# Where the bias row of the feed-forward residual is added: VectorE behind its multiplication, or GpSimd

## The chip, the cores and the metric

The kernel runs on one NeuronCore of a Trainium2 chip. The metric is the device time of one execution in microseconds. The engines are named as the profile names them: PE is TensorE (matmul), PEld its weight loads, DVE is VectorE, ACT is ScalarE, POOL is GpSimd, SP is SyncE, which issues most DMAs.

## What is computed

Two decoder layers on 1024 tokens of 1024 features, float32. The change touches the residual that goes into the second half of each layer, the feed-forward block (FFN). The reference, cut to it:

```python
for i in range(DEPTH):                                   # DEPTH = 2
    ...                                                  # mix: pooling + gating, or short convolution
    x = layer_norm(DEEPNORM_ALPHA * x + mix, ln1_g[i], ln1_b[i])
    hid = jnp.square(jax.nn.relu(jnp.einsum('bsd,df->bsf', x, ffn_w1[i])))   # 1024 -> 4096
    x = layer_norm(DEEPNORM_ALPHA * x + jnp.einsum('bsf,fd->bsd', hid, ffn_w2[i]), ln2_g[i], ln2_b[i])
    gate = jax.nn.sigmoid(jnp.einsum('bsd,de->bse', x, ple_gate_w[i]))
    x = x + gate * jnp.einsum('bsk,kd->bsd', p[i], ple_w[i])
```

`DEEPNORM_ALPHA * x` with `x = norm * ln1_g + ln1_b` is what the tile `resid` must hold before the products with `ffn_w2` are added to it: first `resid * (alpha * gain)`, then `+ (alpha * bias)`.

## The kernel before

**Precision.** Every float32 operand of a product is split into a high part, rounded by ScalarE, and a low part, the difference, made by GpSimd (for weights) or VectorE (for activations). A product is then three matmuls: high by high, high by low, low by high (lines 1597 to 1599).

**The FFN's first product in trips.** The hidden width is worked off in 16 blocks of 256 features. Blocks 0 and 1 are computed plainly. For the blocks 2 to 15 there is one trip each, in which a block of 2 by 2 products is got from seven products instead of eight: A11, S1, A22, S2, A12, S4, S3 (the tuple `PER_TRIP`), where A22 in a trip belongs to the block before. A's take a quarter of `ffn_w1` as it is loaded (`w_raw`), S's take sums and differences of quarters (`op_sum`). Each product is 12 matmuls of 512 columns on PE.

The weight operand of each product passes these hands, four products ahead of PE (`OP_LEAD`), in five slots (`OPERANDS`):

- DVE makes the sums for S1 (line 1260) and S3 (line 1263); POOL makes those for S2 (line 942) and S4 (line 949)
- ACT rounds each operand to its high part `op_hi` (line 1087)
- POOL subtracts to get the low part `op_lo` (line 876, in `operand_low`)
- PE waits for the semaphore `op_low`, then multiplies

Behind PE, ACT copies some results out of PSUM (lines 1097, 1103, 1109), and DVE adds the rest, squares (line 1273) and forms the sums of the hidden tiles that are spilled to DRAM for the second product (lines 1288, 1312, 1314, 1316, 1278).

**What sets the order.** Each engine walks the same list of stages, made by `make_plan`, in program order, and waits on counting semaphores. Nothing is reordered at run time: what stands behind a waiting instruction on its engine waits too. POOL's order in one trip, by operands, with b the block of the products on PE: low A12(b); sum S4(b), low S2(b), low S4(b); low S3(b); low A11(b+1); low A22(b); sum S2(b+1), low S1(b+1).

**The stage "affine".** In the first eight trips of a layer, behind the product A22, one stage "affine" works on one of the eight tiles of 128 tokens of `resid` (128 partitions by 1024 columns). DVE multiplies it with the gain row (`gb_rows[:, 0, :]`, line 1461) and raises the semaphore `gained`; POOL waits for `gained`, adds the bias row (`gb_rows[:, 1, :]`, line 922) and raises `acc_ready`. On POOL this stands between low S3(b) and low A11(b+1). On DVE it stands between the fourth hidden sum (line 1288) and the addition of S2's product from PSUM (line 1292), behind which comes the sum for the next S1 (line 1260). `acc_ready` is waited for much later: by SP before it loads operands of the second product, and by DVE before the first flush into `resid`.

There are 16 such pairs, eight in each layer. The other trips, six in each layer, have none.

Of the kernel before, what the change touches and what calls it, by code (L numbers as in the profile page):

```python
# [26 lines left out]
ALU = mybir.AluOpType  # L27
# [5 lines left out]
TT = SEQ // P  # L33
# [422 lines left out]
def trunk(nc, x, p, ev_w_in, ev_pool_w, ev_pool_scale, ev_sgu_ln_g, ev_sgu_ln_b, ev_sgu_w, ev_sgu_b, ev_w_out,  # L456
# [8 lines left out]
    with ExitStack() as ctx:  # L465
# [19 lines left out]
        resid = at("resid", [P, TT, D], 0)  # L485
# [9 lines left out]
        gb_rows = at("gb_rows", [P, 2, D], 192 * K1)  # L495
# [92 lines left out]
        gained = sem("gained")  # L588
        gb_scaled = sem("gb_scaled")
        acc_ready = sem("acc_ready")  # L590
# [258 lines left out]
        @block.gpsimd  # L849
        def _(pool):  # L850
            pool.memset(ident[:, :], 0.0).then_inc(ident_step, 1)
            pool.wait_ge(ident_step, 1)
            pool.affine_select(out=ident[:, :], in_=ident[:, :], compare_op=ALU.not_equal, fill=1.0, base=0,
                               pattern=[[-1, P]], channel_multiplier=1).then_inc(ident_step, 1)
            def split_low(slab, piece, count):
                for q in range(count):
                    n = piece + q

                    pool.wait_ge(hi_split, n + 1)
                    s = slice(q * PIECE, (q + 1) * PIECE)  # L860
                    pool.tensor_tensor(w_lo[slab % 2][:, s], raw[:, n % NRAW, :], w_hi[slab % 2][:, s].bitcast(F32),  # L861
                                       ALU.subtract).then_inc(lo_split, 1)

            def operand_free(tr, j):

                if j >= OPERANDS:
                    pool.wait_ge(trip_done, tr.slot_before(j))
                else:
                    name, value = ends[trips.index(tr)]["blk0" if j < 4 else "blk1"]
                    pool.wait_ge(sem_of[name], value)  # L870

            def operand_low(tr, b, op):
                s = tr.index[b, op] % OPERANDS
                src = op_sum[s] if op[0] == "S" else None
                pool.wait_ge(op_high, tr.hi[b, op])
                pool.tensor_tensor(by_four(op_lo[s]), by_four(src) if src is not None else w1_quarter(b, op),  # L876
                                   by_four(op_hi[s]).bitcast(F32), ALU.subtract).then_inc(op_low, 1)

            def t_lows(layer, k):
                for m in range(2):  # L880
                    pool.wait_ge(t_high, 8 * layer + 2 * {0: 0, 2: 1, 1: 2, 3: 3}[k] + m + 1)
                    pool.tensor_tensor(pair_of(t_lo[k], m), pair_of(t_raw[k], m), pair_of(t_hi[k], m).bitcast(F32),
                                       ALU.subtract).then_inc(t_low, 1)

            split_low(0, 0, 4)
            pool.wait_ge(param_in, 16 * 7)

            pool.affine_select(out=ws_n, in_=ws_n, compare_op=ALU.is_ge, fill=0.0, base=0,
                               pattern=[[0, 4], [-1, P]], channel_multiplier=1).then_inc(ident_step, 1)

            def stage(st):
                if st.split_next and st.cur + 1 < n_slabs:
                    nxt = slabs[st.cur + 1]
                    split_low(st.cur + 1, st.piece, 5 if nxt[0][0] == "gate" else 4)
                if st.kind == "prep":
                    a, i = ahead[st.layer], st.item
                    k = a.slot(i)
                    pool.wait_ge(ahead_hi, a.act[i] - 1)
                    pool.tensor_tensor(hop_lo[k][:, :, :], h_raw[a.load(i)[0]][:, :, :],  # L899
                                       hop_hi[k][:, :, :].bitcast(F32), ALU.subtract).then_inc(ahead_pool, 1)  # L900
                    o = i % len(ORDER)
                    if i < len(ORDER) * PAIRS and o in SUM_OF:
                        pool.wait_ge(ahead_hi, a.act[i])
                        pool.tensor_tensor(wop_lo[k][:, :, :], w_sum[SUM_OF[o]][:, :, :],  # L904
                                           wop_hi[k][:, :, :].bitcast(F32), ALU.subtract).then_inc(ahead_pool, 1)
                if st.kind == "alpha":

                    pool.wait_ge(sem_of[st.turned[st.half][0]], st.turned[st.half][1])
                    for k in range(HT):
                        t = st.half * HT + k  # L910
                        pool.tensor_scalar(resid[:, t, :], resid[:, t, :], ALPHA, 1.0, ALU.mult, ALU.mult)\
                            .then_inc(acc_ready, 1)
                if st.kind == "stats" and st.half == 0 and st.ln % 2 == 0:

                    pool.wait_ge(gb_in, 32 * (st.ln + 2))
                    pool.tensor_scalar(gb_rows[:, :, :], gb_rows[:, :, :], ALPHA, 1.0, ALU.mult, ALU.mult)\
                        .then_inc(gb_scaled, 1)
                if st.kind == "affine":
                    for t in st.tiles:

                        pool.wait_ge(gained, st.ln // 2 * TT + t + 1)
                        pool.tensor_tensor(resid[:, t, :], resid[:, t, :], gb_rows[:, 1, :], ALU.add)\
                            .then_inc(acc_ready, 1)
                if st.kind == "thi":
                    pool.wait_ge(t_summed, 8 * st.layer + 4)
                    for k in (0, 2):
                        t_lows(st.layer, k)
                if st.kind == "t4":
                    pool.wait_ge(t_summed, 8 * st.layer + 8)
                    for k in (1, 3):  # L930
                        t_lows(st.layer, k)
                if st.kind == "step":
                    tr, j = trips[st.layer], st.item + OP_LEAD
                    if j < len(tr.seq):
                        b, op = tr.seq[j]
                        s = j % OPERANDS
                        if op == "S2":
                            operand_free(tr, j)
                            pool.wait_ge(w1_in[b % 2], w1_landed(st.layer, b))
                            pool.wait_ge(sum_by_dve, tr.sum_dve[b, "S1"])  # L940
                            s1 = op_sum[tr.index[b, "S1"] % OPERANDS]
                            pool.tensor_tensor(by_four(op_sum[s]), by_four(s1), w1_quarter(b, "A11"), ALU.subtract)\
                                .then_inc(sum_by_pool, 1)
                            pool.wait_ge(sum_by_pool, tr.sum_pool[b, "S2"])
                            operand_low(tr, b, "S1")
                        elif op == "S4":
                            operand_free(tr, j)
                            s2 = op_sum[tr.index[b, "S2"] % OPERANDS]
                            pool.tensor_tensor(by_four(op_sum[s]), w1_quarter(b, "A12"), by_four(s2), ALU.subtract)\
                                .then_inc(sum_by_pool, 1)  # L950
                            pool.wait_ge(sum_by_pool, tr.sum_pool[b, "S4"])
                            operand_low(tr, b, "S2")
                            operand_low(tr, b, "S4")
                        elif op != "S1":
                            operand_low(tr, b, op)

            for st in plan:
                stage(st)
# [207 lines left out]
        def _(dve):  # L1166
# [38 lines left out]
            def stage(st):  # L1205
# [9 lines left out]
                if st.kind == "ffn":  # L1215
                    for k in range(2):

                        dve.wait_ge(act_value, st.aval_at + k + 1)
                        t = h_tile[2 * st.half + k][:, :]
# [150 lines left out]
                if st.kind == "fold":  # L1370
                    dve.wait_ge(flushed, st.flu)
                    for k in range(HT):
                        r = resid[:, k, HALF:D]
                        dve.tensor_tensor(r, r, common[:, k, :], ALU.add).then_inc(flushed, 1)

                if st.kind in ("out", "wide"):
                    if st.kind == "wide":
                        dve.wait_ge(flushed, st.flu)
                    for k in range(2 * len(st.tiles)):
                        t, n = st.tiles[k // 2], k % 2  # L1380
                        r = resid[:, t, n * HALF:(n + 1) * HALF]
# [54 lines left out]
                if st.kind == "stats":  # L1436
# [11 lines left out]
                    for k in range(2, HT):  # L1448
                        r = resid[:, h * HT + k, :]
# [3 lines left out]
                if st.kind == "affine":  # L1453
                    for t in st.tiles:
                        if t == 0:
                            dve.wait_ge(gb_in, 32 * (st.ln + 2))
                            dve.wait_ge(gb_scaled, st.ln // 2 + 1)

                        dve.wait_ge(sem_of[st.turned[t // HT][0]], st.turned[t // HT][1])
                        r = resid[:, t, :]  # L1460
                        dve.tensor_tensor(r, r, gb_rows[:, 0, :], ALU.mult).then_inc(gained, 1)  # L1461

                if st.kind == "mix":
                    if st.half == 0 and st.blk == 0:
                        dve.wait_ge(late_in, 32)
                    for k in range(2):
                        t = tmp[:, (st.unit + k) % NTMP, :]
# [79 lines left out]
                if st.kind == "bgate":  # L1547
                    for k in range(2):
                        t = tmp[:, (st.unit + k) % NTMP, :]
# [296 lines left out]
```

## Time and profile before

| what | value |
|---|---|
| time, median of 3 runs | 2288.95 us (2286.92 to 2289.67) |
| time of the profiled execution | 2288.88 us |
| its span, first to last instruction | 2287.1 us |
| PE busy | 2144.5 us (94%) |
| DVE busy | 1577.0 us (69%) |
| POOL busy | 1174.4 us (51%) |
| ACT busy | 660.6 us (29%) |

The span is what the trace covers; the time of an execution has 1.8 us more around it. A share of busy time is a mean over stages with different limits. A timeline row gives an instruction's start, its duration and, in brackets, how long its engine had sat idle before it and who released it. An engine may start an instruction a little before the one ahead has ended. A duration counts from the start to the end also where the instruction was held up in between by another engine.

### The profile page before, as it was taken

How to read it: one execution, taken by the hardware profiler on the slowest of the kernel's cores; microseconds unless marked ns; L12 is line 12 of the kernel's file. 1: busy time of each engine (PE TensorE's matmuls, PEld its weight loads, DVE VectorE, ACT ScalarE, POOL GpSimd, SP SyncE). 2: the span in 40 equal slices, each digit the busy share in tenths (PEclk: the TensorE clock that was granted, in tenths of full speed). 3: DMA queues.
4: the chain of work that ended last, by engine and by line, in shares of the span. 5: the costliest groups of instructions: out<-in, count | busy, mean ns of one | idle time of the engine just before them, and what ended most of it. 6: DMA issues, size and time to landing. Idle time of an engine off the chain costs nothing. (4 is left out here: it accounts for less than half of the span.)

```text
span 2287.1 us, 27876 instructions
## 1 busy us (share of the span) xinstructions
PE 2144.5 (94%) x10581; PEld 1811.5 (79%) x10581; DVE 1577.0 (69%) x2061; ACT 660.6 (29%) x989; POOL 1174.4 (51%) x631
## 2 busy tenths in 40 slices
PE   8999879999969999999999999979999879999999
PEld 8877667777857888899888888757778668888899
DVE  4844777988877777675543353769888788778664
ACT  3111432222333333331211111532222233333421
POOL 4222167887657777122321222267877577776030
PEclk9999999999989999999999999989999989999999
DMA  5111023444454443211121111024434454343112
GB/s 172 37 56 56 19 69 111 148 143 148 157 194 146 166 139 113 76 47 42 38 65 46 56 38 55 28 70 143 145 126 156 153 200 168 138 166 97 37 48 78
DMA packets 150018, 233.87 MB, mean 102 GB/s; under 512 B 11169, under 2 KB 80893, under 8 KB 149885
## 3 DMA queue, kind: packets, MB, share of 16 engines
q1 hardware_dynamic: 149184, 231.78, 29.9%
q8 instruction: 84, 1.38, 0.2%
q14 instruction: 50, 0.40, 0.1%
q10 hardware_dynamic: 700, 0.31, 0.1%
HBM read 172.28 MB, written 59.77 MB: 101 GB/s over the span
## 5 line engine op out<-in xcount | busy, mean ns | idle before, releaser
L861 POOL TENSOR_TENSOR w_lo<-raw,w_hi 128x512 fp32r<-128x512 f32 x160 | 234.5, 1497 | 727.0 <-ACT w_hi L970 726.7
L899 POOL TENSOR_TENSOR hop_lo<-h_raw,hop_hi 128x1024 fp32r<-128x1024 f32 x106 | 291.2, 2764 | 57.2 <-ACT hop_hi L1057 57.2
L1597 PE MATMUL bank_a<-xt_hi,w_hi 128*128 128x512 f32 x640 | 251.6, 393 | 4.2 <-DVE xt_lo L1193 4.1
L1599 PE MATMUL bank_a<-xt_hi,w_lo 128*128 128x512 f32 x640 | 249.5, 390 | 0.0
L1598 PE MATMUL bank_a<-xt_lo,w_hi 128*128 128x512 f32 x640 | 249.4, 390 | 0.0
L876 POOL TENSOR_TENSOR op_lo<-op_sum,op_hi 128x512 fp32r<-128x512 f32 x112 | 182.3, 1638 | 45.3 <-ACT op_hi L1087 40.9
L1597 PE MATMUL bank_b<-wop_hi,hop_hi 128*128 128x512 f32 x464 | 182.6, 394 | 23.1 <-DVE h_tile1b L1281 18.8
L1597 PE MATMUL bank_b<-w_hi,xt_hi 128*128 128x256 f32 x640 | 185.7, 290 | 13.4 <-DVE shared L1575 10.0
L904 POOL TENSOR_TENSOR wop_lo<-w_sum,wop_hi 128x1024 fp32r<-128x1024 f32 x56 | 141.8, 2531 | 106.0 <-ACT wop_hi L1063 106.0
L1597 PE MATMUL bank_a<-wop_hi,hop_hi 128*128 128x512 f32 x448 | 179.6, 401 | 17.6 <-DVE resid L1368 12.0
L1598 PE MATMUL bank_b<-w_lo,xt_hi 128*128 128x256 f32 x640 | 184.1, 288 | 0.0
L1599 PE MATMUL bank_b<-w_hi,xt_lo 128*128 128x256 f32 x640 | 183.9, 287 | 0.0
L1599 PE MATMUL bank_b<-wop_hi,hop_lo 128*128 128x512 f32 x464 | 181.7, 392 | 0.0
L1598 PE MATMUL bank_b<-wop_lo,hop_hi 128*128 128x512 f32 x464 | 181.7, 392 | 0.0
L1087 ACT CAST op_hi<-op_sum 128x512 fp32r<-128x512 f32 x112 | 69.6, 621 | 379.4 <-DVE op_sum L1260 126.2
L1598 PE MATMUL bank_a<-wop_lo,hop_hi 128*128 128x512 f32 x448 | 178.2, 398 | 0.0
L970 ACT CAST w_hi<-raw 128x512 fp32r<-128x512 f32 x160 | 88.2, 620 | 311.5 <-PE bank_a L1599 154.7
L1599 PE MATMUL bank_a<-wop_hi,hop_lo 128*128 128x512 f32 x448 | 177.7, 397 | 0.0
L876 POOL TENSOR_TENSOR op_lo<-w_raw,op_hi 128x512 fp32r<-128x512 f32 x84 | 131.4, 1565 | 49.4 <-ACT op_hi L1087 49.3
L1597 PE MATMUL bank_b<-w_hi,hid_hi 128*128 128x512 f32 (+1 forms) x384 | 140.1, 365 | 11.3 <-DVE resid L1397 5.4
L1597 PEld LDWEIGHTS bank_a<-xt_hi,w_hi 128*128 128x128 f32 x640 | 120.2, 188 | 30.5 <-issue 4.3
L1599 PEld LDWEIGHTS bank_a<-xt_hi,w_lo 128*128 128x128 f32 x640 | 120.2, 188 | 25.0
(175 smaller groups left out, 5384.7 us busy)
## 6 DMA issues: line engine op xcount, KB each, us to landing
h_raw<-h_spill SPq DMA_DIRECT2D x106, 512.0 KB, 3.7
h_spill<-h_tile SPq DMA_DIRECT2D x198, 256.0 KB, 2.0
w_raw<-in_ffn_w_dram SPq DMA_DIRECT2D x64, 512.0 KB, 5.4
w_raw<-in_ffn_w_dram SPq DMA_DIRECT2D x112, 256.0 KB, 3.5
raw<-in_od_w_in_dram SPq DMA_DIRECT2D x48, 256.0 KB, 2.8
raw<-in_ple_gate_w_dram SPq DMA_DIRECT2D x32, 256.0 KB, 3.1
raw<-in_ev_w_in_dram SPq DMA_DIRECT2D x24, 256.0 KB, 3.1
resid<-in_x_dram SPq DMA_DIRECT2D x8, 512.0 KB, 8.8
```

The source lines that it names most:

```text
L861: pool.tensor_tensor(w_lo[slab % 2][:, s], raw[:, n % NRAW, :], w_hi[slab % 2][:, s].bitcast(F32), ALU.subtract).then_inc(lo_split, 1)
L876: pool.tensor_tensor(by_four(op_lo[s]), by_four(src) if src is not None else w1_quarter(b, op), by_four(op_hi[s]).bitcast(F32), ALU.subtra ...
L899: pool.tensor_tensor(hop_lo[k][:, :, :], h_raw[a.load(i)[0]][:, :, :], hop_hi[k][:, :, :].bitcast(F32), ALU.subtract).then_inc(ahead_pool, 1)
L904: pool.tensor_tensor(wop_lo[k][:, :, :], w_sum[SUM_OF[o]][:, :, :], wop_hi[k][:, :, :].bitcast(F32), ALU.subtract).then_inc(ahead_pool, 1)
L970: act.copy(w_hi[slab % 2][:, q * PIECE:(q + 1) * PIECE], raw[:, n % NRAW, :]).then_inc(hi_split, 1)
L1087: act.copy(by_four(op_hi[s]), src).then_inc(op_high, 1)
L1597: pe.matmul(dst, s_hi, m_hi, start=first, stop=False, skip_group_check=on_top)
L1598: pe.matmul(dst, s_hi, m_lo, start=False, stop=False, skip_group_check=on_top)
L1599: return pe.matmul(dst, s_lo, m_hi, start=False, stop=last, skip_group_check=on_top)
```

## The change

POOL's part of the stage "affine" is taken out, and DVE issues the same addition right behind its multiplication. Both raise the same semaphores as before; DVE now waits for its own `gained`, since the addition reads what the multiplication wrote.

```diff
@@ gpsimd, stage @@
-                if st.kind == "affine":
-                    for t in st.tiles:
-
-                        pool.wait_ge(gained, st.ln // 2 * TT + t + 1)
-                        pool.tensor_tensor(resid[:, t, :], resid[:, t, :], gb_rows[:, 1, :], ALU.add)\
-                            .then_inc(acc_ready, 1)
@@ vector, stage @@
                         dve.wait_ge(sem_of[st.turned[t // HT][0]], st.turned[t // HT][1])
                         r = resid[:, t, :]
                         dve.tensor_tensor(r, r, gb_rows[:, 0, :], ALU.mult).then_inc(gained, 1)
+                        dve.wait_ge(gained, st.ln // 2 * TT + t + 1)
+                        dve.tensor_tensor(r, r, gb_rows[:, 1, :], ALU.add).then_inc(acc_ready, 1)
```

DVE around the first such stage, before. The names are tiles, with the number of the buffer: `h_tile` is a hidden tile, `op_sum` the sum of weight quarters.

```order
L1281 TENSOR_TENSOR h_tile_80<-h_tile_80,bank_b 128x512
L1273 SCALAR_TENSOR_TENSOR h_tile_80<-h_tile_80 128x512
L1288 TENSOR_TENSOR h_tile_85<-h_tile_80,h_tile_84 128x512
L1461 TENSOR_TENSOR resid<-resid,gb_rows 128x1024
L1292 TENSOR_TENSOR h_tile_81<-h_tile1b,bank_b 128x512
L1260 TENSOR_TENSOR op_sum_111<-w_raw_112 128x512
L1295 TENSOR_TENSOR h_tile_79<-h_tile_79 128x512
```

And with the change (the file's lines are numbered six lower here):

```order
L1275 TENSOR_TENSOR h_tile_80<-h_tile_80,bank_b 128x512
L1267 SCALAR_TENSOR_TENSOR h_tile_80<-h_tile_80 128x512
L1282 TENSOR_TENSOR h_tile_85<-h_tile_80,h_tile_84 128x512
L1455 TENSOR_TENSOR resid<-resid,gb_rows 128x1024
L1457 TENSOR_TENSOR resid<-resid,gb_rows 128x1024
L1286 TENSOR_TENSOR h_tile_81<-h_tile1b,bank_b 128x512
L1254 TENSOR_TENSOR op_sum_111<-w_raw_112 128x512
L1289 TENSOR_TENSOR h_tile_79<-h_tile_79 128x512
```

The addition (L1457) has come in between the multiplication and the rows that lead to the sum for S1 (`op_sum_111`). Nothing else on DVE has moved.

POOL at the same place, before. The first two rows are low S4 and low S3 of the trip (of `op_sum_108` and `op_sum_109`).

```order
L876 TENSOR_TENSOR op_lo_103<-op_sum_108,op_hi_98 128x512
L876 TENSOR_TENSOR op_lo_104<-op_sum_109,op_hi_99 128x512
L922 TENSOR_TENSOR resid<-resid,gb_rows 128x1024
L876 TENSOR_TENSOR op_lo_105<-w_raw_112,op_hi_100 128x512
L876 TENSOR_TENSOR op_lo_102<-w_raw_113,op_hi_97 128x512
L942 TENSOR_TENSOR op_sum_108<-op_sum_111,w_raw_112 128x512
```

And with the change:

```order
L876 TENSOR_TENSOR op_lo_103<-op_sum_108,op_hi_98 128x512
L876 TENSOR_TENSOR op_lo_104<-op_sum_109,op_hi_99 128x512
L876 TENSOR_TENSOR op_lo_105<-w_raw_112,op_hi_100 128x512
L876 TENSOR_TENSOR op_lo_102<-w_raw_113,op_hi_97 128x512
L936 TENSOR_TENSOR op_sum_108<-op_sum_111,w_raw_112 128x512
L876 TENSOR_TENSOR op_lo_106<-op_sum_111,op_hi_101 128x512
```

The row of `resid` is gone; low S3 (`op_lo_104<-op_sum_109`) is now followed at once by low A11 (`op_lo_105<-w_raw_112`). The orders of ACT, PE and SP are what they were.

## Rows read from the trace of the kernel before

**Rows 1.** Groups by line; busy us, mean ns of one.

```profile
L922 POOL TENSOR_TENSOR resid<-resid,gb_rows 128x1024 f32<-128x1024 f32 x16 | 38.3, 2394 | 28.2 <-DVE resid L1461 28.2
...
L1461 DVE TENSOR_TENSOR resid<-resid,gb_rows 128x1024 f32<-128x1024 f32 x16 | 19.4, 1211 | 0.0
```

**Rows 2.** Waits; PE, eight trips of layer 0, then of layer 1.

```profile
PE bank_a L1597 <- POOL op_lo L876: 12.7, 8, 1.7
...
PE bank_a L1597 <- POOL op_lo L876: 12.8, 8, 1.7
```

**Rows 3.** Timeline of DVE, one trip; start us, duration us, [idle before].

```profile
411.57 1.66 DVE L1288 TENSOR_TENSOR h_tile<-h_tile,h_tile 128x512 f32<-128x512 f32 x1
413.15 1.21 DVE L1461 TENSOR_TENSOR resid<-resid,gb_rows 128x1024 f32<-128x1024 f32 x1
414.29 0.67 DVE L1292 TENSOR_TENSOR h_tile<-h_tile1b,bank_b 128x512 f32<-128x512 f32 x1
414.89 2.50 DVE L1260 TENSOR_TENSOR op_sum<-w_raw 128x512 f32<-128x512 f32 x1
...
422.86 1.54 DVE L1312 TENSOR_TENSOR h_tile<-h_tile,h_tile 128x512 f32<-128x512 f32 x1
424.43 1.67 DVE L1314 TENSOR_TENSOR h_tile<-h_tile,h_tile 128x512 f32<-128x512 f32 x1
...
428.48 1.02 DVE L1278 TENSOR_TENSOR h_tile<-h_tile,h_tile 128x512 f32<-128x512 f32 x1 [0.68 <-ACT h_tile L1103]
```

**Rows 4.** Timeline of POOL, the same trip.

```profile
411.00 1.68 POOL L876 TENSOR_TENSOR op_lo<-op_sum,op_hi 128x512 fp32r<-128x512 f32 x1 [1.33 <-ACT op_hi L1087]
414.44 2.40 POOL L922 TENSOR_TENSOR resid<-resid,gb_rows 128x1024 f32<-128x1024 f32 x1 [1.76 <-DVE resid L1461]
416.80 1.74 POOL L876 TENSOR_TENSOR op_lo<-w_raw,op_hi 128x512 fp32r<-128x512 f32 x1
419.18 1.30 POOL L876 TENSOR_TENSOR op_lo<-w_raw,op_hi 128x512 fp32r<-128x512 f32 x1 [0.64 <-ACT op_hi L1087]
...
422.25 1.60 POOL L876 TENSOR_TENSOR op_lo<-op_sum,op_hi 128x512 fp32r<-128x512 f32 x1
423.81 1.74 POOL L876 TENSOR_TENSOR op_lo<-w_raw,op_hi 128x512 fp32r<-128x512 f32 x1
...
431.98 1.68 POOL L876 TENSOR_TENSOR op_lo<-op_sum,op_hi 128x512 fp32r<-128x512 f32 x1 [1.34 <-ACT op_hi L1087]
```

**Rows 5.** Timeline of ACT, the same trip.

```profile
410.83 0.62 ACT L1087 CAST op_hi<-w_raw 128x512 fp32r<-128x512 f32 x1
417.48 0.62 ACT L1087 CAST op_hi<-op_sum 128x512 fp32r<-128x512 f32 x1 [6.03 <-DVE op_sum L1260]
...
418.50 0.61 ACT L1087 CAST op_hi<-w_raw 128x512 fp32r<-128x512 f32 x1
...
427.34 0.62 ACT L1087 CAST op_hi<-op_sum 128x512 fp32r<-128x512 f32 x1 [3.45 <-POOL op_sum L949]
427.86 0.58 ACT L1103 COPY h_tile<-bank_a 128x512 f32<-128x512 f32 x1
```

**Rows 6.** Timeline of PE, the same trip, and a restart elsewhere.

```profile
99.92 0.50 PE L1597 MATMUL bank_b<-w_hi,hid_hi 128*128 128x512 f32 x1 [2.49 <-DVE resid L1394]
...
424.00 0.47 PE L1597 MATMUL bank_a<-t_hi,op_hi 128*128 128x512 f32 x1 [1.67 <-POOL op_lo L876]
```

**Rows 7.** Timeline of DVE and POOL, 1024 columns each, second products.

```profile
669.71 3.30 DVE L1334 TENSOR_TENSOR w_sum<-w_raw 128x1024 f32<-128x1024 f32 x1
...
669.53 2.40 POOL L899 TENSOR_TENSOR hop_lo<-h_raw,hop_hi 128x1024 fp32r<-128x1024 f32 x1
```

**Rows 8.** Stretches: us, busy of PE, PEld, DVE, ACT, POOL, clock, DMA.

```profile
540.00:635.00 95.00, 94.67 (x415) 77.28 (x413) 77.79 (x71) 27.49 (x45) 65.25 (x40) 1.00 0.46 163
100.60:104.00 3.40, 3.40 (x10) 2.62 (x9) 1.74 (x3) 0.00 (x0) 0.00 (x0) 0.50 0.00 0
424.00:427.40 3.40, 3.40 (x15) 2.81 (x16) 3.33 (x3) 0.06 (x1) 3.32 (x3) 1.00 0.89 304
```

## The prediction

> **What bounds the kernel now.** First, who adds the bias row, and for how long: POOL, 16 times, 2.39 us each; the multiplication ahead of it takes DVE 1.21 us [rows 1]. The table of waits then says whether the trips with this stage are PE's: they are not. In each of the two layers PE waits eight times, together 12.7 and 12.8 us, each time for POOL's low part `op_lo` (L876) before it starts S1, the second product of a trip [rows 2, 6]. In the trips without the stage there is no such wait: PE is busy for 94.67 of 95.00 us [rows 8]. So the trips with the stage are limited by the engines that prepare PE's operands, and a change of their pace shows in the time without a discount.
>
> The timelines of one such trip give the ring that sets this pace. Read them by asking of each row what released it:
>
> - POOL starts low S3 at 411.00 and ends it at 412.68 [rows 4].
> - DVE starts L1288 at 411.57 but needs 1.66 us for what takes some 0.7 us elsewhere, and ends at 413.23, 0.55 behind POOL's end [rows 3, 4]. That is the signature of a resource that one of the two engines holds at a time: a DVE instruction that reads two tiles in SBUF starts its work only when POOL's running one has ended, and ends 0.55 us later at 512 columns. L1312 does the same: POOL's row ends at 422.25 + 1.60 = 423.85, DVE's at 424.40. The other way round, POOL's next low (issued 423.81) ends at 425.55, 1.15 behind DVE's 424.40, and L1314 0.55 behind that, at 426.10. The two take turns.
> - The multiplication L1461 runs 413.15 to 414.36. POOL idles meanwhile (1.76 us), since its next instruction is the addition that waits for it [rows 4].
> - POOL adds, 414.44 to 416.84. L1292 reads PSUM and runs beside it, 0.67 us. L1260, the sum for the next S1, reads two tiles in SBUF: issued at 414.89, it ends at 417.39, again 0.55 behind POOL [rows 3].
> - ACT rounds S1 at 417.48 and A22 at 418.50, POOL idles 0.64 us for the latter, then makes low A22, sum S2 and low S1, which ends at 423.85; PE starts S1 at 424.00 [rows 4 to 6].
> - POOL's sum S4 releases ACT (427.34), ACT's copy of S1's result (427.86) releases DVE's L1278 (428.48), behind it stands the sum for S3, which ACT rounds for POOL's next low S3 at 431.98 [rows 3 to 5].
>
> The ring is closed after 431.98 - 411.00 = 20.98 us, and every row in it is released by the one before. PE isn't in it, except as the one that waits 1.67 us.
>
> **The change step by step.** All of it lies between L1288's end (413.23) and L1260's end (417.39), 4.16 us of the ring.
>
> *Removed:* the addition on POOL. L1260 was held up until 0.55 us behind its end, 1.82 us more than its own work: with POOL idle it should take 0.68 us (2.50 - 0.68 = 1.82; 0.68 is the duration of the equally wide DVE rows that nothing holds, as L1292's 0.67 [rows 3]).
>
> *Moved up:* POOL's low A11 no longer stands behind the addition. Its high part is ready since 410.83 + 0.62 = 411.45 [rows 5], so POOL issues it when low S3 ends, and is in line while DVE still runs L1288. By the turns above it goes next: it ends 1.15 behind 413.23, at 414.38. The multiplication, issued at 413.15, is now the one that is held. What a row of 1024 columns needs once POOL lets go is in another stage: a POOL row ends at 669.53 + 2.40 = 671.93, the DVE row issued at 669.71 ends at 673.01, 1.08 later [rows 7]. So the multiplication ends at 414.38 + 1.08 = 415.46, 1.10 us later than now.
>
> *Added:* DVE's wait for itself and the addition. L1314 waits in the same manner for L1312 and starts 0.03 us behind its end (424.40 to 424.43); without a wait a row starts 0.08 us early (L1461 at 413.15) [rows 3]. So the wait costs some 0.1 us, and the addition runs from 415.49. It isn't in the trace on DVE; same width, same tiles, another operation: 1.21 us [rows 1] when nothing holds it. POOL could hold it only with its next instruction, low A22, and that waits for ACT, which waits in order behind S1's high part, so for L1260. POOL is idle then. The addition ends at 416.70.
>
> *Behind it:* L1292 from 416.63 to 417.30, L1260 from 417.23 to 417.91.
>
> Sum: 417.91 - 417.39 = **0.52 us later per trip**. POOL gets 2.4 us of work less and idles for it. ACT's rounding of A22 comes 0.52 later too, POOL is waiting for it, and from there on each step of the ring moves as a whole, so the trip becomes 21.5 us. PE's wait grows from 1.67 to 2.19 us. What is queued on DVE behind the new wait is L1292 and L1260, and ACT, POOL and at last PE wait for the latter. The first of the eight waits of a layer is shorter than the rest (12.7 less seven of 1.67 leaves 1.0), but above zero, so it grows by the same. Nothing takes it up later: the next stages start from PE's last products and from rows that move along. SP waits for `acc_ready` only trips later, so an earlier or later addition costs it nothing, and its weight loads follow POOL's low A22 and move with it.
>
> 16 x 0.52 = 8.3 us. The profiled execution took 2288.88 us, its span 2287.1; that is 0.1 off the median of 2288.95, so I add to it as it is: **2297.2 us**.
>
> Of the self-wait there is another price. The Trainium skill (VectorE: DVE Perf Modes, section The DRAIN you can't avoid) says that a semaphore between two VectorE instructions costs nothing extra, as they run one after the other anyway. By it the addition would start 0.11 us sooner and the time would be 2295.5 us; the rows L1312 and L1314 show the 0.11, and I go by them.
>
> **The rivals.**
>
> *Faster.* The multiplication isn't held by low A11, because `resid` and `gb_rows` don't meet POOL's operands, or since the hold-up of the rows above has another cause. Then it takes 1.21 us, from 413.15 to 414.36, the addition ends at 415.60, L1260 at 416.81: 0.58 us sooner per trip, 9.3 in all, **2279.6 us**. The two instructions together decide: from L1288's side, L1260 ends at 413.15 plus both durations plus 1.24, so up to 3.00 us for the two the change gains, and I expect 2.31 + 1.21 = 3.52. For it speaks that every multiplication of the trace took 1.21 us; but POOL was idle in each, by the order of the program. Against it, that all held rows end 0.54 to 0.56 behind POOL's, whatever tiles they read, and at 1024 columns too.
>
> The Trainium skill (GPSIMD Engine Reference, section 4.1 Engine selection) gives this change its reason: an elementwise addition belongs on VectorE, GpSimd being some two times slower with two inputs. The rows agree, 2.39 against 1.21 us. Taken alone it would promise the faster case; it leaves out that the addition was also what POOL did while DVE had L1292 to do, and that low A11 now collides with the multiplication.
>
> *No change.* DVE gets its turn for both instructions before POOL's low A11, since it issues them 0.03 to 0.08 us apart. Then low A11 starts at 415.60 and ends at 416.75, L1260 is held until 417.30: 0.09 sooner per trip, 2287.5 us. Against it: where POOL was in line first, it went first. If DVE wins only the first turn, low A11 comes between the two, the addition ends at 416.59 and L1260 at 417.80: 0.41 later per trip, 2295.4 us, inside the forecast.
>
> *Slower by more.* PE's clock falls. Behind a wait of 2.49 us PE's granted clock was 0.50, its level of 1.2 GHz, in the stretch from 100.6 to 104.0, with 10 matmuls in it; behind the 1.67 us wait here it stayed at 1.00, 2.4 GHz, with 15 [rows 6, 8]. A wait of 2.19 lies between. Five matmuls of 0.23 us are 1.1 us per fall. S1's result would come up to 1.1 us later; its last matmul ends near 427.0 now and ACT reads it at 427.86, so 0.9 of it is covered and some 0.25 per trip lengthens the ring: up to 4 us in all, and up to 1.1 per layer at the end. That gives 2299 to **2303 us**.
>
> **Chances and range.** Forecast, with its variant at 2295.4: 0.62. The clock besides: 0.14. No change: 0.12. Faster: 0.12. A measurement of this kernel tells some 0.2% (4.6 us) from no change, so slower by more than that has 0.76, within it 0.12, faster 0.12. The range reaches from the case of no change, 2287.5, to the clock's upper end and a little over it for a ring that I have mispriced by a tenth of a microsecond a trip, 2304; the faster case is left out.
>
> **What the new profile would show.** If right: 16 multiplications of about 2.3 us and 16 additions of 1.2 us on DVE; the sum for S1 at 0.68 in place of 2.50 us; low A11 at 1.74 us directly behind low S3, and POOL idle for some 5 us before low A22; trips of 21.5 us; PE's eight waits per layer at 2.2 us, about 17 us together in place of 12.7. Multiplications of 1.21 us with low A11 beside them show the faster case, low A11 drawn out to over 4 us that of no change, matmuls of 0.34 us behind S1's start the clock. The prediction is wrong too if the sum for S1 comes 0.52 us later and PE's wait doesn't grow, which would mean a slack in the ring that I don't see.

## The result

| | median us | lowest to highest | runs |
|---|---|---|---|
| before | 2288.24 | 2284.53 to 2289.67 | 6 |
| with the change | 2298.85 | 2292.36 to 2300.49 | 6 |

The ratio is 1.0042, with a 95% interval of 1.0028 to 1.0057: 9.6 us slower, between 6.4 and 13.0 (the two medians by themselves are 10.6 apart). 2297.2 us was predicted.

The profiled execution of the changed kernel took 2292.36 us, the lowest of the six. By the time PE waits for the first S operand, ahead of all that is changed, it is 4.3 us ahead of the profiled execution of before. Here is that wait of PE after and, below it, before (start, duration, idle time ahead):

```profile
342.22 0.77 PE L1593 MATMUL bank_b<-t_hi,op_hi 128*128 128x512 f32 x1 [15.83 <-POOL op_lo L876]
```

```profile
346.54 0.77 PE L1597 MATMUL bank_b<-t_hi,op_hi 128*128 128x512 f32 x1 [15.82 <-POOL op_lo L876]
```

So the two spans can't be subtracted as they are. Counted from this wait on, the changed kernel's execution is 7.8 us longer (2290.6 less 2287.1 plus 4.3). The traces are read by the trip. The changed instructions after, by lines of the program (L1455 multiplies, L1457 adds, L1254 makes the sums for S1; busy us, mean ns of one), which answer to [rows 1]:

```profile
L1455 DVE TENSOR_TENSOR resid<-resid,gb_rows 128x1024 f32<-128x1024 f32 x16 | 36.9, 2307 | 0.0
...
L1254 DVE TENSOR_TENSOR op_sum<-w_raw 128x512 f32<-128x512 f32 x28 | 23.2, 828 | 11.9 <-DMA w_raw<-in_ffn_w_dram 11.9
...
L1457 DVE TENSOR_TENSOR resid<-resid,gb_rows 128x1024 f32<-128x1024 f32 x16 | 19.6, 1226 | 0.6
```

The multiplication takes 2.31 us in place of 1.21, the addition 1.23, the sum 0.83 on the mean in place of 1.87. POOL's busy time fell from 1174.4 to 1135.5 us, DVE's rose from 1577.0 to 1585.7:

```profile
PE 2144.5 (94%) x10581; PEld 1805.7 (79%) x10581; DVE 1585.7 (69%) x2077; ACT 660.6 (29%) x989; POOL 1135.5 (50%) x615
```

One trip after, on DVE, which answers to [rows 3]:

```profile
409.56 1.67 DVE L1282 TENSOR_TENSOR h_tile<-h_tile,h_tile 128x512 f32<-128x512 f32 x1
411.15 2.31 DVE L1455 TENSOR_TENSOR resid<-resid,gb_rows 128x1024 f32<-128x1024 f32 x1
413.49 1.23 DVE L1457 TENSOR_TENSOR resid<-resid,gb_rows 128x1024 f32<-128x1024 f32 x1
414.63 0.68 DVE L1286 TENSOR_TENSOR h_tile<-h_tile1b,bank_b 128x512 f32<-128x512 f32 x1
415.23 0.69 DVE L1254 TENSOR_TENSOR op_sum<-w_raw 128x512 f32<-128x512 f32 x1
```

On POOL, which answers to [rows 4]:

```profile
408.99 1.68 POOL L876 TENSOR_TENSOR op_lo<-op_sum,op_hi 128x512 fp32r<-128x512 f32 x1 [1.34 <-ACT op_hi L1081]
410.64 1.73 POOL L876 TENSOR_TENSOR op_lo<-w_raw,op_hi 128x512 fp32r<-128x512 f32 x1
417.70 1.30 POOL L876 TENSOR_TENSOR op_lo<-w_raw,op_hi 128x512 fp32r<-128x512 f32 x1 [5.33 <-ACT op_hi L1081]
...
430.52 1.69 POOL L876 TENSOR_TENSOR op_lo<-op_sum,op_hi 128x512 fp32r<-128x512 f32 x1 [1.33 <-ACT op_hi L1081]
```

The trip is 430.52 - 408.99 = 21.53 us long, against 20.98. Low A11 follows low S3 at once and ends at 412.37; the multiplication, issued at 411.15, ends at 413.46, 1.09 behind it. The sum for S1 ends at 415.92, 4.69 us behind the end of L1282 (411.23); before, that stretch was 4.16. POOL is idle for 5.33 us until ACT, waiting behind that sum, has rounded A22.

PE's waits in the eight trips of layer 0, which answer to [rows 2] (total us, times, longest; those of layer 1 are 11.3 and 3.6 us):

```profile
PE bank_a L1593 <- POOL op_lo L876: 11.3, 8, 1.4
PE bank_b L1593 <- DVE h_tile L1286: 3.5, 7, 0.5
```

In the timeline of PE, the same trip, ahead of S3:

```profile
414.46 0.39 PE L1595 MATMUL bank_a<-xt_hi,op_lo 128*128 128x512 f32 x1
415.36 0.50 PE L1593 MATMUL bank_b<-t_hi,op_hi 128*128 128x512 f32 x1 [0.52 <-DVE h_tile L1286]
```

And ahead of S1:

```profile
422.53 0.47 PE L1593 MATMUL bank_a<-t_hi,op_hi 128*128 128x512 f32 x1 [1.42 <-POOL op_lo L876]
```

PE waits in two places now. Before S1 it is 1.42 us, less than the 1.67 of before. The other is new: 0.52 us ahead of 415.36, where S3 starts, for DVE's L1286. Together they are 1.94.

### The profile page after: what moved, and what is told of

Read it like the earlier page. It is cut to its first block and busy times, and to the rows that moved or that the text cites. A ratio compares the mean times of both kernels' runs of the same rounds, so it can differ in the third digit from the quotient of the medians.

```text
span 2290.6 us, 27876 instructions
## 1 busy us (share of the span) xinstructions
PE 2144.5 (94%) x10581; PEld 1805.7 (79%) x10581; DVE 1585.7 (69%) x2077; ACT 660.6 (29%) x989; POOL 1135.5 (50%) x615
## 5 line engine op out<-in xcount | busy, mean ns | idle before, releaser
L1593 PE MATMUL bank_b<-wop_hi,hop_hi 128*128 128x512 f32 x464 | 183.2, 395 | 23.7 <-DVE h_tile1b L1275 18.8
```

Of the source, the lines that this page charges most:

```text
L1593: pe.matmul(dst, s_hi, m_hi, start=first, stop=False, skip_group_check=on_top)
```

## The experiments

Nine kernels, each beside runs of the kernel before on the same chip. The ratio is to those, with its 95% interval; the trip is the distance of one sum for S1 from the next in the middle of the changed trips.

| kernel | median us | ratio (interval) | trip us |
|---|---|---|---|
| before | 2287.6 to 2288.4 | 1 | 20.98 |
| the change | 2298.85 | 1.0042 (1.0028 to 1.0057) | 21.53 |
| no_bias | 2274.64 | 0.9947 (0.9930 to 0.9963) | 20.28 |
| add_twice | 2315.42 | 1.0124 (1.0109 to 1.0140) | 22.78 |
| pool_waits_gain | 2286.62 | 0.9994 (0.9985 to 1.0004) | 20.93 |
| pool_add_behind_low | 2308.67 | 1.0086 (1.0071 to 1.0101) | 22.29 and 22.09 in turn |
| pair_behind_s2 | 2286.96 | 0.9999 (0.9990 to 1.0008) | 20.93 |
| bias_of_tile_before | 2293.18, one run | none | 21.40 |
| pair_behind_sum | 2266.27 | 0.9909 (0.9892 to 0.9926) | 19.62 |
| spread_over_trips | 2258.68 | 0.9875 (0.9861 to 0.9890) | 18.8 and 19.6, mean 19.09 |
| gain_behind_sum_pool_adds | 2273.39 | 0.9936 (0.9920 to 0.9953) | 20.03 |

The theory is the ring of the prediction: POOL, DVE and ACT release each other once around in every trip, whatever stands on DVE between the fourth hidden sum (L1288 before, L1282 after) and the sum for S1 counts in full, and DVE and POOL take turns at one resource that both need for reading two tiles in SBUF. The main rival is that the load of DVE alone is what counts.

### Is the addition on the ring?

The kernel no_bias leaves the bias row out of the result, add_twice counts it twice (its semaphore `twice` is declared with the others).

```diff
@@ no_bias: vector, stage "affine" @@
-                        dve.tensor_tensor(r, r, gb_rows[:, 0, :], ALU.mult).then_inc(gained, 1)
-                        dve.wait_ge(gained, st.ln // 2 * TT + t + 1)
-                        dve.tensor_tensor(r, r, gb_rows[:, 1, :], ALU.add).then_inc(acc_ready, 1)
+                        dve.tensor_tensor(r, r, gb_rows[:, 0, :], ALU.mult).then_inc(acc_ready, 1)
@@ add_twice: vector, stage "affine" @@
-                        dve.tensor_tensor(r, r, gb_rows[:, 1, :], ALU.add).then_inc(acc_ready, 1)
+                        dve.tensor_tensor(r, r, gb_rows[:, 1, :], ALU.add).then_inc(twice, 1)
+                        dve.wait_ge(twice, st.ln // 2 * TT + t + 1)
+                        dve.tensor_tensor(r, r, gb_rows[:, 1, :], ALU.add).then_inc(acc_ready, 1)
```

> The changed kernel without the addition: the bias row is left out of the residual, nothing else. Ring theory: the multiplication is still held by low A11 (2.31 us), the sum for S1 ends 1.25 us sooner than with the change and 0.7 sooner than before: trips of 20.3 us, 20 us less than with the change, 2277 to 2279. Rival (the addition on DVE is hidden, and only the hold-up costs): about 2298 us, as with the change.

> The changed kernel with the addition done twice on DVE, each waiting for the one before, so the bias counts double in the residual. Ring theory: all of the second addition lies on the ring while POOL idles beside it, 1.24 us per trip: trips of 22.8 us, 20 us more than with the change, 2317 to 2320. PE's wait before S3 grows by the same, from 0.68 to 1.9 us, that before S1 stays. Rival (a slack takes part of it): less than 10 us more.

Measured: without the addition the trip is 20.28 us, with it 21.53, with two 22.78: 1.25 us for each, its 1.23 us and the start behind its predecessor. All of it is on the ring. The two times are 40.8 us apart, 20.4 for each addition of a trip, as expected; but both are some 2 us below their expected ranges, which were reckoned from the changed kernel's median. The middle between them, 2295.0 us, lies in the lower part of that kernel's own interval (1.0028 is 2294.6 us). If both steps are equal, this points to a cost of the change of 7 to 9 us rather than 10 or more; its trips give 8.8 and its execution from the first wait on 7.8. PE's waits with two additions, layer 0 (the table ends at 545 us and misses the eighth wait before S1; with it they are 11.3 us):

```profile
PE bank_b L1596 <- DVE h_tile L1287: 13.3, 8, 1.7
PE bank_a L1596 <- POOL op_lo L877: 9.9, 7, 1.4
```

It is the wait before S3 that took the 1.2 us (it is up to 1.7 us, where it was up to 0.5), while that before S1 stayed at 1.4. The expectation's 0.68 and 1.9 us for the same wait count from where PE's next matmul would have started, the profile from the modelled end of the last one. The new wait of PE is thus caused by S2's addition (L1286), which now stands behind the pair.

### Is the multiplication held by POOL's low A11?

```diff
@@ pool_waits_gain: the changed kernel; gpsimd, stage @@
+                if st.kind == "affine":
+                    for t in st.tiles:
+                        pool.wait_ge(gained, st.ln // 2 * TT + t + 1)
@@ pool_add_behind_low: the kernel before; gpsimd, stage @@
-                if st.kind == "affine":
-                    for t in st.tiles:
-
-                        pool.wait_ge(gained, st.ln // 2 * TT + t + 1)
-                        pool.tensor_tensor(resid[:, t, :], resid[:, t, :], gb_rows[:, 1, :], ALU.add)\
-                            .then_inc(acc_ready, 1)
...
                         elif op != "S1":
                             operand_low(tr, b, op)
+                    if st.item >= 0 and tr.seq[st.item][1] == "S2":
+                        t = tr.seq[st.item][0] - 1 - PLAIN
+                        if 0 <= t < TT:
+                            pool.wait_ge(gained, st.layer * TT + t + 1)
+                            pool.tensor_tensor(resid[:, t, :], resid[:, t, :], gb_rows[:, 1, :], ALU.add)\
+                                .then_inc(acc_ready, 1)
```

> The changed kernel, but POOL still waits for the multiplication before low A11, without anything to add. Ring theory with turns: the multiplication isn't held (1.21 us in place of 2.31), the addition is in line before low A11 and goes first, low A11 then holds the sum for S1: 1.8 us in place of 0.69. Trips of 20.9 us, time 2286 to 2288, back at the kernel before though POOL does less and waits more. Rival (the multiplication's 2.31 us are a matter of VectorE itself): it stays at 2.31 and the time at 2298.

> The kernel before, with the addition on POOL, but behind low A11 instead of ahead of it. Ring theory: the multiplication is held by low A11 (2.31 us), POOL's addition starts 1.1 us later and still holds the sum for S1 until its end: trips of 22.1 us, 16 to 18 us more than before, 2304 to 2307 us. PE's wait before S1 nears 2.8 us, and its clock may fall to 0.5 behind it. Rival (who adds decides, not the order on POOL): 2288 us.

Measured: with nothing but a wait added on POOL, the changed kernel's median is 12 us lower (by its trips, 0.60 us each, it is 9.6) and level with the kernel before. DVE in one of its trips:

```profile
412.47 1.21 DVE L1458 TENSOR_TENSOR resid<-resid,gb_rows 128x1024 f32<-128x1024 f32 x1
413.72 1.23 DVE L1460 TENSOR_TENSOR resid<-resid,gb_rows 128x1024 f32<-128x1024 f32 x1
414.86 0.68 DVE L1289 TENSOR_TENSOR h_tile<-h_tile1b,bank_b 128x512 f32<-128x512 f32 x1
415.46 1.18 DVE L1257 TENSOR_TENSOR op_sum<-w_raw 128x512 f32<-128x512 f32 x1
```

POOL, low A11 in the same trip:

```profile
413.76 2.33 POOL L876 TENSOR_TENSOR op_lo<-w_raw,op_hi 128x512 fp32r<-128x512 f32 x1 [1.77 <-DVE resid L1458]
```

The multiplication is back at 1.21 us. The addition was issued 0.04 us ahead of low A11 and goes first, low A11 is held to 2.33 us, and holds the sum for S1 in its turn. That one takes 1.18 us, where the expectation had 1.8; its end, 0.55 us behind low A11's, and the trip of 20.93 us are as expected.

In pool_add_behind_low the multiplication takes 2.31 us though the addition is POOL's as before. That settles that the hold-up comes from POOL's order and not from what DVE does itself. Its time, 2308.7, is 1.7 us over the expected range. PE's waits before S1 alternate between 1.40 and 2.74 us there (the first of a layer is 2.12 or 2.21), and the clock with them. One of the long waits:

```profile
424.70 0.47 PE L1597 MATMUL bank_a<-t_hi,op_hi 128*128 128x512 f32 x1 [2.74 <-POOL op_lo L876]
```

And the stretches behind it and behind the next, short wait, with the columns of [rows 8] (0.51 and 1.00 are the granted clock):

```profile
425.50:428.90 3.40, 3.40 (x10) 2.62 (x9) 2.95 (x2) 0.62 (x1) 3.32 (x3) 0.51 0.81 299
447.50:450.90 3.40, 3.40 (x16) 2.81 (x16) 3.29 (x2) 0.54 (x2) 3.32 (x3) 1.00 0.84 303
```

Ten matmuls against 16 in 3.4 us: the clock fell to its lower level, 1.2 GHz, behind the wait of 2.74 us, S1's result came later, that trip was longer by what of it wasn't covered, and PE's lateness shortened its next wait to 1.40 us, behind which the clock stayed up. By the sum for S1, the trips with a fall are 22.29 us long and those without 22.09, so a fall costs 0.2 us. The eight falls of the two layers make 1.6 us, about what the time is over its range. Measured from one sum for S3 to the next, the trips seem to be 23.28 and 21.12 us. But behind a fall that sum only starts later, and isn't held then (0.68 us in place of 1.78), so that it ends 22.2 us behind the one before every time. A trip is best measured at a row that doesn't change its own length.

### Does the place decide?

Two kernels with both instructions on DVE at other places. The multiplication and the addition are put into two functions, `gain` and `add_bias`, with the same waits and semaphores, and the stage "affine" is taken out of DVE.

```diff
@@ pair_behind_s2: vector, stage "step", behind S2's addition from PSUM @@
                             dve.tensor_tensor(c12, c21, bank, ALU.add).then_inc(hid_step, 1)
+                            if 0 <= b - 1 - PLAIN < TT:
+                                gain(st, b - 1 - PLAIN)
+                                add_bias(st, b - 1 - PLAIN)
@@ pair_behind_sum: vector, stage "step", behind the sums for S1 and S3 @@
+                    if st.item >= 0 and tr.seq[st.item][1] == "A12":
+                        t = tr.seq[st.item][0] - 1 - PLAIN
+                        if 0 <= t < TT:
+                            gain(st, t)
+                            add_bias(st, t)
                     if st.item >= 0:
                         b, op = tr.seq[st.item]
```

> Both on DVE, behind S2's addition and ahead of the sum for S1. Ring theory: S2's addition reads PSUM, runs beside low A11 in the time in which the multiplication would be held, so 0.6 us of it costs nothing: trips of 20.9 us, the time of the kernel before less 1 to 2 us, 2286 to 2288. PE no longer waits for DVE before S3, its whole wait is before S1, 1.6 to 1.8 us. Rival (the time is lost because S2's addition comes late for PE's S3): the same gain from that side, but then PE's wait before S1 would stay at 1.4 us and the trip would be shorter by the 0.68 us of the wait before S3. Rival (DVE's load alone): 2295 to 2300 us.

> Both instructions on DVE, but issued behind the sum for the next S1 instead of ahead of S2's addition. Ring theory (the ring of POOL, DVE and ACT sets the trip; what stands between the fourth hidden sum and the sum for S1 counts in full): the sum for S1 is held only by low A11 and ends some 2.5 us sooner than in the kernel before; multiplication and addition fill the stretch in which DVE waits for ACT (1.24 us idle) and POOL for ACT, and cost only what is left over, some 0.5 us. Trips of 19.0 to 19.6 us, near PE's own 19.04, in place of 20.98 before and 21.53 with the change; time 2260 to 2268 us. Rival (DVE has too much to do in these trips, the place doesn't matter): 2295 to 2300 us as with the change.

Measured: one place further on, behind S2's addition, and the loss is gone (20.93 us a trip, 2286.96 us). S2's addition reads PSUM and isn't held, so it now passes in the time in which the multiplication would only stand in line; that one takes 1.72 us on the mean. PE waits before S1 alone, 12.3 us in eight, 1.59 to 1.65 each but for the first. The rival that S2's addition was too late for PE's S3 wanted 1.4 there, and is out by that; the lengths of the trips hardly part the two (0.60 us shorter, where it had 0.68). One place further still, behind the sum for S1, and the kernel is 20.8 us faster than before (trips of 19.62 us, at the upper end of what was expected). DVE in one of its trips:

```profile
408.34 1.67 DVE L1298 TENSOR_TENSOR h_tile<-h_tile,h_tile 128x512 f32<-128x512 f32 x1
409.93 0.68 DVE L1302 TENSOR_TENSOR h_tile<-h_tile1b,bank_b 128x512 f32<-128x512 f32 x1
410.53 1.18 DVE L1265 TENSOR_TENSOR op_sum<-w_raw 128x512 f32<-128x512 f32 x1
411.63 1.21 DVE L1204 TENSOR_TENSOR resid<-resid,gb_rows 128x1024 f32<-128x1024 f32 x1
412.88 1.23 DVE L1208 TENSOR_TENSOR resid<-resid,gb_rows 128x1024 f32<-128x1024 f32 x1
414.02 1.78 DVE L1305 TENSOR_TENSOR h_tile<-h_tile 128x512 f32<-128x512 f32 x1
```

The sum for S1 (L1265) ends at 411.71, 1.70 us behind the end of the fourth hidden sum at 410.01, in place of 4.69. ACT goes on from there, and both instructions run while DVE would wait for ACT anyway. What is left over is that the addition holds POOL's low A22, and that one the next DVE row, L1305, 1.78 us in place of 0.69. Work of DVE is the same in all three kernels; the rival that its load decides is out.

### Is the self-wait free?

```diff
@@ bias_of_tile_before: vector, stage "step"; the stage "affine" is gone as above @@
+                        if op == "A22":
+                            t = b - PLAIN
+                            if t < TT:
+                                gain(st, t)
+                            if 1 <= t <= TT:
+                                add_bias(st, t - 1)
```

> The changed kernel, but in each trip DVE multiplies tile t and adds the bias to tile t-1, so that the addition doesn't wait for the instruction right ahead of it; one more trip has an addition alone. Look at the start of the addition against the end of the multiplication. As the rows of before have it: 0.08 us ahead of it in place of 0.03 behind, and trips shorter by 0.1 us. By the Trainium skill (VectorE: DVE Perf Modes, section The DRAIN you can't avoid), which says that the semaphore costs nothing: trips as with the change, 21.53 us.

Measured, DVE in one trip:

```profile
410.18 2.31 DVE L1204 TENSOR_TENSOR resid<-resid,gb_rows 128x1024 f32<-128x1024 f32 x1
412.41 1.21 DVE L1208 TENSOR_TENSOR resid<-resid,gb_rows 128x1024 f32<-128x1024 f32 x1
413.55 0.67 DVE L1303 TENSOR_TENSOR h_tile<-h_tile1b,bank_b 128x512 f32<-128x512 f32 x1
```

The multiplication ends at 412.49 and the addition starts at 412.41, 0.08 us ahead of it; with the change it started 0.03 behind. The trips are 21.40 us long, 0.13 shorter. The addition has its wait here too, but for something long done. The Trainium skill (VectorE: DVE Perf Modes, section The DRAIN you can't avoid) reports of a chain of `tensor_copy` instructions that a semaphore behind each "costs nothing extra". These float32 rows of 1024 columns differ: waiting for the instruction right ahead, whose tile the addition reads, costs 0.11 to 0.13 us each time. Whether the wait costs that or the reading of a tile just written isn't separated here. (The time of the single run tells nothing, it lies among those of the changed kernel.)

### A version that beats both

```diff
@@ spread_over_trips: vector @@
+            PER_BLOCK = (1, 1, 2, 1, 1, 2, 1, 1, 2, 1, 1, 1, 1, 0)
...
+                    if st.item >= 0 and tr.seq[st.item][1] == "A12":
+                        done = sum(PER_BLOCK[:tr.seq[st.item][0] - PLAIN])
+                        for i in range(done, done + PER_BLOCK[tr.seq[st.item][0] - PLAIN]):
+                            (add_bias if i % 2 else gain)(st, i // 2)
@@ gain_behind_sum_pool_adds: the kernel before, with gain(st, t) on DVE as in pair_behind_sum, without add_bias; gpsimd, stage "step" @@
+                    if st.item >= 0 and tr.seq[st.item][1] == "A22":
+                        t = tr.seq[st.item][0] - 1 - PLAIN
+                        if 0 <= t < TT:
+                            pool.wait_ge(gained, st.layer * TT + t + 1)
+                            pool.tensor_tensor(resid[:, t, :], resid[:, t, :], gb_rows[:, 1, :], ALU.add)\
+                                .then_inc(acc_ready, 1)
```

> As pair_behind_sum, but the 16 instructions of a layer are dealt over 13 trips (one behind the sum for S1 in ten trips, two in three), multiplication and addition of a tile mostly in different trips. Ring theory: one instruction of 1.21 us fits the 1.24 us for which DVE waits for ACT there, so these trips become PE's own: 19.04 us in place of 19.63, no wait of PE before S1. That is some 6 us less than pair_behind_sum, 2259 to 2262 us. Rival (any instruction more costs its length, wherever it stands): as pair_behind_sum, 2266 us.

> The multiplication on DVE behind the sum for S1, the addition on POOL as before, one trip later and ahead of low S3, where POOL waits for ACT. It asks whether VectorE is the better engine for the addition once the place is right. Ring theory: POOL idles for 1.3 us there and adds 2.4, so low S3 comes some 1 us late, and DVE's sum for S3 is held: trips of 20.0 us against 19.63 with the addition on DVE, 2272 to 2276 us. Rival (POOL's time is free wherever it waits): no more than pair_behind_sum, 2266 us.

Measured: dealt out over 13 trips, the two instructions make PE wait for nothing. These are all of PE's waits that the table has from 340 to 640 us, all 14 trips of layer 0:

```profile
PE bank_b L1599 <- POOL op_lo L876: 15.8, 1, 15.8
PE bank_b L1599 <- DVE h_tile1b L1292: 9.4, 1, 9.4
```

The first is the wait for the first S operand that the other kernels have too, the second comes behind the last trip. The time is 2258.68 us, 1.25% under the kernel before, 1.7% under the change and 0.3 us below the expected range. With the multiplication behind the sum for S1 and the addition left on POOL, ahead of low S3, the trip is 20.03 us, and POOL's addition takes 2845 ns on the mean in place of 2394, held by DVE. So, of the places tried, VectorE is the better engine for the addition after all, by 0.4 us a trip (2266.3 against 2273.4 us), once it stands where DVE has time. Other places on POOL weren't tried.

## Why the prediction was right, and where it wasn't

The time was right: 2297.2 forecast, 2298.85 measured as a median, and 9.6 us (6.4 to 13.0) of difference where 8.3 was the sum. The account of PE's waits wasn't right, and that the clock stayed up may be luck. By its steps:

- *That the trips with the stage are a ring of POOL, DVE and ACT.* Shown by no_bias, add_twice, pair_behind_sum and spread_over_trips: 1.25 us a trip per addition at the old place, no wait of PE at a place with slack.
- *Multiplication held, 1.10 us.* 2.31 us in all 16, as forecast; pool_waits_gain takes the hold-up away with a wait alone, and pool_add_behind_low brings it into the kernel before.
- *The addition, 1.21 us, unheld.* 1.23.
- *The self-wait, 0.03 behind in place of 0.08 ahead.* As forecast, and bias_of_tile_before shows its price.
- *The sum for S1 at 0.68 us, 1.82 less.* 0.69.
- *Sum, 0.52 a trip.* 0.55 (21.53 against 20.98), 8.8 us in 16 trips. The 0.03 more is the addition's 1.23 for 1.21 and rounding.
- *POOL idle for some 5 us before low A22.* 5.33.
- *PE's wait before S1 grows from 1.67 to 2.19 us.* **Wrong.** It fell to 1.42, and PE got a second wait, 0.52 us by the profile, before S3. The step that failed is the sentence on what is queued behind the pair: I named L1292 and L1260 and let PE wait "at last for the latter" alone. But PE's S3 adds on top of the bank that S2's addition (L1292, L1286 after) has first to read, so it waits for that one too. Before, that row ended at 414.96 [rows 3], 1.76 us ahead of PE's first matmul of S3; the pair moved it by 2.3 us and used that up. For the sum it makes no difference, since the ring doesn't pass through PE's S3: what PE loses there it waits less before S1. add_twice and pair_behind_s2 show both sides of it. The prediction had named this as a sign of being wrong: the sum for S1 comes 0.5 us later and the wait before S1 doesn't grow. It meant a slack in the ring; there is none (the trips are 0.55 longer), and what it had overlooked is the second wait. Together the two are 1.94 us, in a layer 14.8, where 2.19 and 17 were forecast. The first wait of a layer, which should have grown by the same as the rest, went from 1.04 to 1.42.
- *The clock rival.* It didn't come. In the stretch behind S1's start the clock was at 1.00, and so it was on the mean over all changed trips:

```profile
422.50:425.90 3.40, 3.37 (x15) 2.83 (x16) 3.33 (x3) 0.03 (x1) 3.32 (x3) 1.00 0.90 300
```

But it stayed up behind waits of 0.52 and 1.42 us, not behind the single one of 2.19 that was forecast, so this part came out for a reason that the prediction didn't have. In the traces of the kernel before, the change, add_twice and pool_add_behind_low, from 100 us on, the 3.4 us behind each wait of 1.2 to 1.92 us are at 1.00. From there on it goes either way. The waits of 2.12 and 2.21 us in pool_add_behind_low brought the clock down, one of 2.29 in the changed kernel, in another stage, didn't:

```profile
380.30 0.47 PE L1597 MATMUL bank_a<-t_hi,op_hi 128*128 128x512 f32 x1 [2.12 <-POOL op_lo L876]
380.30:383.70 3.40, 3.40 (x10) 2.68 (x11) 3.33 (x3) 0.08 (x1) 3.32 (x3) 0.63 0.89 296
```

```profile
656.19 0.47 PE L1593 MATMUL bank_b<-wop_hi,hop_hi 128*128 128x512 f32 x1 [2.29 <-DVE resid L1362]
656.19:659.59 3.40, 3.40 (x15) 2.81 (x16) 3.40 (x5) 1.36 (x2) 0.23 (x1) 1.00 1.04 403
```

So a wait of 2.19 us could well have brought it down; that the split kept it up is argued, not tested. The rival's price is shown: 0.25 us a trip forecast for a fall, 0.2 measured in pool_add_behind_low, where it came in every other trip.

The matmul on which the missed wait rests, the first of S3 in the kernel before:

```profile
416.72 0.39 PE L1597 MATMUL bank_b<-t_hi,op_hi 128*128 128x512 f32 x1
```

The other rivals are out by the rows: no multiplication of 1.21 us beside low A11 (faster), no low A11 drawn out to 4 us (no change; in pool_waits_gain, where it is made to happen, the time is the forecast one of that case, 2286.6 against 2287.5).

## What to carry to other kernels

Before you move an instruction from one engine to another, look at where it lands: what the engine that it leaves will issue at once in its place, and which of the new neighbours needs what both engines share. Find the stretch in which the receiving engine waits for somebody anyway; here the same two instructions gave trips of 21.53, 20.93 or 19.62 us within three places of each other on the same engine, and 19.09 on the mean, with no wait of PE, when dealt out by one or two to a trip. And list every consumer behind the place, also those whose slack seems ample (here 1.76 us, for a shift of 2.3): a row that slips by more than its slack makes a wait of its own, though it may only take from another.

## What the runs showed of the hardware

- VectorE and GpSimd exclude each other for instructions that read two tiles in SBUF, for the whole instruction, and take turns in the order of issue: a VectorE row of 512 columns ends 0.55 us behind GpSimd's, of 1024 columns 1.08 to 1.09, a GpSimd row of 512 columns 1.14 to 1.15 behind VectorE's. The profile shows the time in line as duration of the one that waits: 2.31 for 1.21 us, 2.33 for 1.3. A VectorE row with one operand in PSUM isn't held. The Trainium skill (SBUF — State Buffer, section Who interferes with whom) states that a VectorE instruction with two inputs in SBUF contends with a GpSimd instruction that reads SBUF, that one with at most one doesn't, and that the order of issue decides who blocks. The traces agree, and add the handing-over times.
- A fall of PE's clock can limit itself: where the wait before a product brings it down, PE's lateness shortens the next wait, and the clock falls in every other trip (pool_add_behind_low: waits of 2.74 and 1.40 us in turn, trips of 22.29 and 22.09).
